# The last layer's key and value projections read x times the norm's weight, and its root enters behind them

## The reference, cut to what matters

```python
def rms_norm_2(x, g):
    xf = x.astype(jnp.float32)
    y = xf * lax.rsqrt(jnp.mean(xf * xf, axis=-1, keepdims=True) + EPS)
    return (y * g.astype(jnp.float32)).astype(x.dtype)

def shared_kv(h, norm_g, w_kv, knorm_g, cos, sin):
    Bsz, S, _ = h.shape
    kv = (rms_norm_2(h, norm_g) @ w_kv).astype(jnp.float32)
    k, v = jnp.split(kv, 2, axis=-1)
    k = k.reshape(Bsz, S, B_KV_HEADS, B_HD)
    v = v.reshape(Bsz, S, B_KV_HEADS, B_HD)
    k = apply_rope(rms_norm_2(k, knorm_g), cos, sin)
    return k, v
...
def dilated_layer(h, k, v, norm_g, w_in, qnorm_g, w_out, cos, sin):
    Bsz, S, _ = h.shape
    proj = rms_norm_2(h, norm_g) @ w_in
    q, z = jnp.split(proj, [B_QW], axis=-1)
```

## Time and profile before

| what | us |
|---|---|
| median of 3 runs (2129.85 to 2136.19) | 2133.31 |
| device time of the profiled execution | 2135.45 |
| its span, first to last instruction | 2133.7 |
| TensorE busy in the span | 1981.5 |
| VectorE busy | 1175.1 |
| ScalarE busy | 847.1 |

### The profile page before, as it was taken

The page is one execution under the profiler, slowest core; times in us unless marked ns, Lnnn a source line. Parts: engine busy times, 40 slices in busy tenths (PEclk is TensorE's granted clock), DMA queues, the critical chain, the costliest instruction groups (busy, mean ns, idle before and its releaser), DMA issues.

```text
span 2133.7 us, 24330 instructions
## 1 busy us (share of the span) xinstructions
PE 1981.5 (93%) x9296; PEld 1630.8 (76%) x9296; DVE 1175.1 (55%) x2051; ACT 847.1 (40%) x1319; POOL 0.2 (0%) x4
## 2 busy tenths in 40 slices
PE   1989988999998998889989999999999999899999
PEld 0866666888886887889877888887887877677877
DVE  8557846665667465466535432435653555655554
ACT  3226713232223533256633231324344534557343
POOL 0000000000000000000000000000000000000000
PEclk7999999999999979589999999999999999899999
DMA  9551053556554222000022222222221132132021
GB/s 357 202 207 41 1 186 140 208 177 214 179 200 154 99 79 79 1 1 1 1 90 79 99 98 98 98 98 79 88 90 60 60 143 79 59 119 79 1 90 59
DMA packets 42216, 223.85 MB, mean 105 GB/s; under 512 B 4444, under 2 KB 5212, under 8 KB 23694
## 3 DMA queue, kind: packets, MB, share of 16 engines
q1 hardware_dynamic: 41602, 222.25, 29.3%
q10 hardware_dynamic: 524, 0.41, 0.1%
HBM read 219.45 MB, written 3.19 MB: 104 GB/s over the span
## 4 chain that ended last, share of the span: by engine, by line
PE 83%; DVE 8%; DMA 4%; ACT 3%; issue 2%; SPq 0%; DVEq 0%; ACTq 0%
PE bank L419 22%; PE bank L421 22%; PE bank L420 22%; PE bank L1554 3%; DMA raw<-wts_d 2%; PE bank L1525 2%; DMA adab<-ada_d 1%; PE bank L1515 1%; PE bank L2701 1%; PE bank L1516 1%; DVE wL L405 1%; DMA ada<-ada_d 1%; DVE tmp L522 1%; PE bank L731 1%; ACT wH L400 1%
## 5 line engine op out<-in xcount | busy, mean ns | idle before, releaser
L419 PE MATMUL bank<-hH,wH 128*128 128x512 f32 x1344 | 536.8, 399 | 65.8 <-DVE hL L531 37.7
L420 PE MATMUL bank<-hL,wH 128*128 128x512 f32 x1344 | 531.3, 395 | 0.0
L421 PE MATMUL bank<-hH,wL 128*128 128x512 f32 x1344 | 531.2, 395 | 0.0
L419 PEld LDWEIGHTS bank<-hH,wH 128*128 128x128 f32 x1344 | 258.2, 192 | 129.8 <-issue 66.7
L996 ACT ACTIVATE wH<-raw 128x2048 fp32r<-128x2048 f32 x64 | 122.7, 1917 | 470.6 <-PE bank L421 470.6
L405 DVE TENSOR_TENSOR wL<-raw,wH 128x2048 fp32r<-128x2048 f32 x76 | 174.0, 2289 | 238.2 <-ACT wH L400 237.9
L420 PEld LDWEIGHTS bank<-hL,wH 128*128 128x128 f32 x1344 | 258.0, 192 | 54.4 <-issue 1.0
L421 PEld LDWEIGHTS bank<-hH,wL 128*128 128x128 f32 x1344 | 257.2, 191 | 54.8
L1040 DVE TENSOR_TENSOR wL<-raw,wH 128x2048 fp32r<-128x2048 f32 x64 | 146.5, 2289 | 228.8 <-ACT wH L996 228.8
L400 ACT ACTIVATE wH<-raw 128x2048 fp32r<-128x2048 f32 x76 | 145.3, 1912 | 259.6 <-PE bank L421 221.3
L419 PE MATMUL bank<-aH,wH 128*128 128x512 f32 x512 | 199.2, 389 | 0.0
(11 more groups left out here) (344 smaller groups left out, 2585.8 us busy)
## 6 DMA issues: line engine op xcount, KB each, us to landing
raw<-wts_d SPq DMA_DIRECT2D x140, 1024.0 KB, 4.9
adab<-ada_d SPq DMA_DIRECT2D x96, 512.0 KB, 4.3
ada<-ada_d SPq DMA_DIRECT2D x4, 2048.0 KB, 22.4
bt<-bias_rows SPq DMA_DIRECT2D x1, 4096.0 KB, 12.7
x<-x_d SPq DMA_DIRECT2D x1, 2048.0 KB, 9.5
peF<-ple_d SPq DMA_DIRECT2D x2, 1024.0 KB, 5.7
out_d<-x SPq DMA_DIRECT2D x4, 512.0 KB, 2.7
pF<-p_d SPq DMA_DIRECT2D x2, 512.0 KB, 3.6
```

The lines of the kernel that those rows point to most:

```text
L419: pe.matmul(o, l[0], r[0], start=start, stop=False)
L420: pe.matmul(o, l[0], r[1], start=False, stop=False)
L421: return pe.matmul(o, l[1], r[0], start=False, stop=stop)
```

## The change

Keys and values are now projected from x times the norm's weight, without the root of the mean square. The root r of a token is a common factor of its key and value. For the keys the norm of each head removes it again, if eps is divided by r squared: the program forms eps times the mean square plus eps squared (`epsK`, one VectorE instruction) and adds it to the head's mean square in place of eps (four VectorE instructions, which read PSUM and write kD). For the values the root is multiplied in where ScalarE copies them out, as a scale per token; for that TensorE transposes the root (four 128x128 transposes) and VectorE copies one column of each into `rtok`. Since the gate projection still reads hH and hL, chunks 4 to 7 of the new operand have a place of their own (k4H, k4L). The mean of the squares is taken after chunk 5 of the key tile, and the query norm's chunks 4 to 7 are applied first.

```diff
+        def xg(c):
+            return (hH[:, c, :], hL[:, c, :]) if c < 4 else (sb["k4H"][:, c - 4, :], sb["k4L"][:, c - 4, :])
+
+        def xg_act(act, c):
+            act.wait_ge(ple_x, c + 1)
+            act.activation(xg(c)[0], x[:, c, :], ACT.Copy, scale=col("norm_kv", c)).then_inc(h_hi, 1)
+
+        def xg_dve(dve, c):
+            dve.wait_ge(h_hi, KC * 7 + c + 1)
+            dve.scalar_tensor_tensor(out=xg(c)[1], in0=x[:, c, :], scalar=col("norm_kv", c),
+                                     in1=xg(c)[0].bitcast(F32), op0=ALU.mult, op1=ALU.subtract).then_inc(h_lo, 1)
...
             hi(act, n + 3)
-            if n + 4 < N_HALF:
+            if l == 0:
                 hi(act, n + 4)
+
+                act.wait_ge(half_used, n + 3)
+                for c in range(4):
+                    xg_act(act, c)
             for m in range(4):
                 o, freed = evac(act, a + 3, m)
                 bank_done(act, DONE0[a + 3], m, n + 4)
                 act.activation(sg[:, 4 + m, :], o, ACT.Sigmoid).then_inc(freed, 1)
-                if l == 0 and m < 3:
-                    sq_act(act, 7, lambda e, c: e.wait_ge(ple_x, c + 1), [m])
-            if n + 4 < N_HALF:
+                if l == 0 and m >= 1:
+                    xg_act(act, 3 + m)
+            if l == 0:
+                xg_act(act, 7)
                 act.preload_act_table_set(EXP_LN)
...
         def act_fourth(act):
-            sq_act(act, 7, lambda e, c: e.wait_ge(ple_x, c + 1), range(3, KC))
-            rstd_act(act, 7, 61)
-            apply_act(act, 7, None, lambda e: hi(e, N_K2 + 1))
+            hi(act, N_K2 + 1)
+            sq_act(act, 7, lambda e, c: e.wait_ge(ple_x, c + 1), range(KC))
             hi(act, N_K2 + 2)
+            rstd_act(act, 7, 60)
+            apply_act(act, 8, None, chunks=range(4, KC))
             hi(act, N_K2 + 3)
             act.wait_ge(half_used, N_K2 + 2)
             head_copy(act, 0)
 
             hi(act, N_DI)
             apply_act(act, 8, None, chunks=range(0, 4))
-            head_rstds(act, 0)
+            for m in range(4):
+                r = kD[:, m, :]
+                act.wait_ge(acc_free[1], 4 * 30 + m + 1)
+                act.activation(r, r, ACT.Ln).then_inc(ln_done, 1)
+                act.wait_ge(ln_done, 8 + m + 1)
+                act.activation(r, r, ACT.Exp, scale=-0.5).then_inc(hn_ex, 1)
             hi(act, N_DI + 1)
-            apply_act(act, 8, None, chunks=range(4, KC))
+            act.wait_ge(rp, 6)
             for m in range(4):
                 o, freed = evac(act, 62, m)
-                act.activation(vD[:, m, :], o, ACT.Copy).then_inc(freed, 1)
+                act.activation(vD[:, m, :], o, ACT.Copy, scale=rtok[:, m:m + 1]).then_inc(freed, 1)
...
         def dve_fourth(dve):
-            sq_dve(dve, 7, range(4, 7))
+            lo(dve, N_K2 + 1)
+            sq_dve(dve, 7, range(1, 7))
...
-            apply_dve(dve, 7, 7, lambda c: col("norm_kv", c), None, lambda e: lo(e, N_K2 + 1))
-            dve.wait_ge(rp, 4)
             lo(dve, N_K2 + 2)
+
+
+            dve.wait_ge(rstd_done, 8)
+            dve.tensor_scalar(sb["epsK"][:, :], bank[:, 0, :], EPS, EPS * EPS, ALU.mult, ALU.add).then_inc(rp, 1)
+            dve.wait_ge(l_t, 9)
+            dve.tensor_copy(rtok, blocks(bank[:, 3, :])[:, :, 0:1].rearrange("p i o -> p (i o)")).then_inc(rp, 1)
+            apply_dve(dve, 8, 7, lambda c: col("norm_b", c), None, chunks=range(4, KC))
+            dve.wait_ge(rp, 5)
             lo(dve, N_K2 + 3)
             head_rope(dve, 0)
             lo(dve, N_DI)
+            for m in range(4):
+                o, freed = evac(dve, 61, m)
+                dve.wait_ge(hn_mm, m + 1)
+                dve.scalar_tensor_tensor(out=kD[:, m, :], in0=o, scalar=float(D // P), in1=sb["epsK"][:, :],
+                                         op0=ALU.mult, op1=ALU.add).then_inc(freed, 1)
             apply_dve(dve, 8, 7, lambda c: col("norm_b", c), None, chunks=range(0, 4))
             head_end(dve, 0)
             lo(dve, N_DI + 1)
-            apply_dve(dve, 8, 7, lambda c: col("norm_b", c), None, chunks=range(4, KC))
             lo(dve, N_DI + 2)
...
         def pe_fourth(pe):
-            stats_pe(pe, 7, 61)
-            tile_mm(pe, 61, N_K2, hbase=56)
-            tile_mm(pe, 62, N_K2 + 2, tok=True, between=lambda: head_pe(pe, 0))
-            tile_mm(pe, 63, N_DI, hbase=64)
+            acc_wait(pe, 61)
+            for j in range(2):
+                pe.wait_ge(w_lo, N_K2 + j + 1)
+                for kk in range(4):
+                    k = 4 * j + kk
+                    pe.wait_ge(h_lo, KC * 7 + k + 1)
+                    for m in range(4):
+                        last = three(pe, bank[:, 4 + m, :], wpart((N_K2 + j) % 2, kk, m * P, P), xg(k), k == 0,
+                                     k == KC - 1)
+                    if k == 5:
+                        stats_pe(pe, 7, 60, 62)
+                last.then_inc(half_used, 1)
+            pe.wait_ge(rstd_done, 8)
+            for i in range(NT):
+                last = pe.transpose(bank[:, 3, i * P:(i + 1) * P], rstd[:, i * P:(i + 1) * P], ident[:, :])
+            last.then_inc(l_t, 1)
...
+            tile_mm(pe, 63, N_DI, hbase=68)
```

More of the change, by code:

```diff
@@ L320, in place @@
     m["dmask"] = nc.alloc_sbuf_tensor_at("dmask", [P, T], F32, offset=m["cw2_at"])
+    t("k4H", [P, 4, T], "bias", 8 * K, F32R)
+    t("k4L", [P, 4, T], "bias", 16 * K, F32R)
+    t("epsK", [P, T], "bias")
     t("rope", [P, 2, T], "misc", 12 * K)
@@ L452, in tile_mm @@
                     if hbase is not None:
-                        pe.wait_ge(h_lo, hbase + 4 * j + kk + 1)
+                        pe.wait_ge(h_lo, min(hbase + 4 * j + kk + 1, KC * 9) if a == 63 else hbase + 4 * j + kk + 1)
                     for m in range(4):
@@ L500, in sq_dve, with stats_pe @@
                 dve.tensor_tensor(sq_slot(0), sq_slot(0), sq_slot(c), ALU.add).then_inc(sq_sum, 1)
-        def stats_pe(pe, s, next_a):
-            acc_wait(pe, next_a)
+        def stats_pe(pe, s, next_a, after=None):
+            acc_wait(pe, after or next_a)
             if s == 0:
@@ L516, in rstd_act, with nth @@
             act.activation(rstd[:, :], bank[:, 4 * (next_a % 2), :], ACT.Ln, bias=one[:, 1:2]).then_inc(ln_done, 1)
-            act.wait_ge(ln_done, s + 1)
+            act.wait_ge(ln_done, s + 1 + (4 if s == 8 else 0))
             act.activation(rstd[:, :], rstd[:, :], ACT.Exp, scale=-0.5).then_inc(rstd_done, 1)
+        TMP0 = [KC * p if p < 8 else KC * (p - 1) for p in range(10)]
+        def nth(p, c):
+            return (c + 4) % KC if p == 8 else c
         def apply_dve(dve, p, s, scale, shift, mid=None, chunks=range(KC)):
             def product(c):
-                dve.scalar_tensor_tensor(out=tmp[:, c % 3, :], in0=x[:, c, :], scalar=scale(c), in1=rstd[:, :],
+                dve.scalar_tensor_tensor(out=tmp[:, nth(p, c) % 3, :], in0=x[:, c, :], scalar=scale(c), in1=rstd[:, :],
                                          op0=ALU.mult, op1=ALU.mult).then_inc(tmp_done, 1)
             def rest(c):
-                dve.wait_ge(h_hi, KC * p + c + 1)
+                dve.wait_ge(h_hi, KC * p + nth(p, c) + 1)
                 if shift is None:
-                    dve.tensor_tensor(hL[:, c, :], tmp[:, c % 3, :], hH[:, c, :].bitcast(F32),
+                    dve.tensor_tensor(hL[:, c, :], tmp[:, nth(p, c) % 3, :], hH[:, c, :].bitcast(F32),
                                       ALU.subtract).then_inc(h_lo, 1)
@@ L536, in slot_wait @@
             def slot_wait(c):
-                if c >= 3:
-                    dve.wait_ge(h_lo, KC * p + c - 2)
+                if nth(p, c) >= 3:
+                    dve.wait_ge(h_lo, KC * p + nth(p, c) - 2)
             for c in chunks[0:2]:
@@ L553, in apply_act @@
             for c in chunks:
-                act.wait_ge(tmp_done, KC * p + c + 1)
+                act.wait_ge(tmp_done, TMP0[p] + nth(p, c) + 1)
                 if shift is None:
-                    act.activation(hH[:, c, :], tmp[:, c % 3, :], ACT.Copy).then_inc(h_hi, 1)
+                    act.activation(hH[:, c, :], tmp[:, nth(p, c) % 3, :], ACT.Copy).then_inc(h_hi, 1)
                 else:
@@ L2440, in ple_dve @@
             lo(dve, n + 3)
-            if n + 4 < N_HALF:
+            if l == 0:
                 lo(dve, n + 4)
+                dve.wait_ge(ple_x, 4)
+                for c in range(4):
+                    xg_dve(dve, c)
             for c in range(4, KC):
                 gated(c)
-                if l == 0 and 5 <= c:
-                    sq_dve(dve, 7, [c - 4])
                 grow(c)
+                if l == 0 and c >= 5:
+                    dve.wait_ge(ple_x, c)
+                    xg_dve(dve, c - 1)
+            if l == 0:
+                dve.wait_ge(ple_x, KC)
+                xg_dve(dve, KC - 1)
         def ple_pe(pe, l, a, n, hbase):
@@ L2662, in head_end @@
                 dve.wait_ge(hn_ex, e + 1)
```

(29 more changed lines are left out.)

## The result

The changed kernel takes 2118.38 us (median of 7 runs, 2112.17 to 2125.03) against 2134.18 us before (7 runs). The ratio is 0.9926, with a 95% interval of 0.9908 to 0.9943: 12 to 20 us faster, 15.8 us between the medians. The forecast was 2119.2 us, 14.1 us less than before. The profiled execution has a span of 2117.5 us, 16.2 less than that of before.

The account below looks back on a forecast made before the run. TensorE was taken as the bound, busy 1981.5 of 2133.7 us, with two stalls. Filling the pause ahead of the keys brings the values' copies and tile 64 14.1 us earlier: 2133.31 - 14.1 = 2119.2 us, range 2114 to 2125.

Parts of the forecast that it names:

- The pause ahead of the keys: Between gate projection and key tile: keys follow at once, at 1814.95 instead of 1829.13, 14.18 us earlier.
- Statistics and transposes at full clock: Around the key tile: two statistics matmuls inside it, 1.73 us, plus four transposes, 0.44, so 2.17 us more.
- TensorE's side to tile 63: First query tile can start on TensorE 13.94 us earlier, at about 1864.3: 14.18 + 1.93 - 2.17.
- The chain to the values' copies: ScalarE and VectorE steps from the key tile's end, 36.2 us: copies end at 1874.65 against 1888.77, 14.1 us earlier.
- The scale per partition in the copies: ScalarE's four value copies: reading a scale per partition adds 4 x 0.087 = 0.35 us to 2.04.
- From the copies to tile 64: From the values' copies' end through two moves and the load: 15.97 us as before, so tile 64 at 1890.6.
- The slow start behind it: Slow matmuls behind tile 64's wait for its weights (some 4.5 us) stay; full clock there would save 1.7 us.
- The rule on transposes: Four transposes before the values: 0.44 us and nothing after by the rows; by the skill's rule possibly a 1.93 us slow start.
- Values' copies not earlier: Rival: the list ahead of the values' copies runs 14 us longer than summed, no change, 2133 us; chance 0.04.
- Slower by the clock: Rival: small waits keep TensorE at 1.2 GHz through key and value tiles, up to 43 us, 2162; chance 0.03.
- A wait inside the key tile: Rival: longer lists run 3 us late, TensorE waits 1 to 3 us in the key tile, 2122 to 2125; chance 0.10.
- Half of the second stall goes: Rival: before tile 64, up to 1.7 us or the whole 4.5 us wait also goes, 2113 to 2117; chance 0.05.

Follow-up runs that it names:

- e1: Changed kernel with the two statistics matmuls ahead of the key tile again, not behind its fifth chunk: ratio 1.0009 to the kernel before, stage 171.71 us.
- e5: Changed kernel with the two statistics matmuls two chunks earlier in the key tile (k == 3 for k == 5): ratio 0.9943 to the kernel before.
- e2: Changed kernel with the load of weight half N_DI+2 issued ahead of the values' move in SP's queue: 2113.11 us, ratio 0.9906 to the kernel before.
- e4: Changed kernel with VectorE's copy of the root per token put behind the query norm's chunks 4 to 7: ratio 0.9899 to the kernel before.
- e3: Kernel before the change, with the load of weight half N_DI+2 issued ahead of the values' move: ratio 0.9983 to the kernel before.
- e7: Changed kernel with both reorderings, e2's earlier load and e4's later root copy: 2112.26 us, ratio 0.9891 to the kernel before.
- e6: Changed kernel with the query norm's chunks 4 to 7 back in their old place, behind weight half N_DI+1: ratio 0.9945 to the kernel before.

## Why the prediction was right, point by point

- **The pause ahead of the keys.** Forecast: gone, 14.18 us. Measured: the last gate matmul and the first key matmul start 0.23 us apart (1812.53 and 1812.76), the pace of full speed. The forecast had let the keys begin behind the end of that last matmul, at 1814.95 on its clock; matmuls overlap (0.39 us long, 0.23 apart), so they came 0.22 us earlier. e1 puts the pause back, and the gain goes with it.
- **Statistics and transposes at full clock, 2.17 us.** From the first key matmul (1812.76) to the first transpose (1836.30) pass 23.54 us, and 96 x 0.2267 + 1.73 = 23.49.
- **TensorE's side to tile 63.** Forecast 60.2 us behind the anchor (1864.3 - 1804.11), measured 1862.00 - 1802.14 = 59.86; 0.22 of the difference is the start of the keys. The waits that the forecast feared where it had no margin did not occur: the last square of the heads was ready 50.2 us behind the anchor (paced: 50.6), the query norm's chunk 0 at 59.3 (paced: 60.0).
- **The chain to the values' copies.** Forecast: they begin 68.1 us behind the anchor. Measured 67.22, 0.87 earlier. Two terms were mis-sized, both for the better. The four pairs of Ln and Exp took 1.19 each, not 1.24; Ln takes 0.62 on kD, where it took 0.67 on PSUM with a second operand (`one`), and no run tells which of the two makes the difference. The four sums from PSUM took 2.39 to the next instruction, 0.60 each, where I had taken 0.66. These two make up 0.45; most of the rest was already there when ScalarE began to round N_DI (50.10 us behind the anchor, forecast 50.5), half of it from the earlier start of the keys. The sums on VectorE, then ScalarE, in the changed kernel:

```profile
1856.39 2.48 DVE L3023 SCALAR_TENSOR_TENSOR kD<-bank,epsK 128x512 f32<-128x512 f32 x4
1858.78 2.07 DVE L532 SCALAR_TENSOR_TENSOR tmp<-x,cols,rstd 128x512 f32<-128x512 f32 x3
...
1862.81 0.62 ACT L2977 ACTIVATE kD<-kD 128x512 f32<-128x512 f32 x1
1863.46 0.63 ACT L2979 ACTIVATE kD<-kD 128x512 f32<-128x512 f32 x1
1863.99 0.62 ACT L2977 ACTIVATE kD<-kD 128x512 f32<-128x512 f32 x1
...
1867.55 1.90 ACT L403 ACTIVATE wH<-raw 128x2048 fp32r<-128x2048 f32 x1
1869.36 2.40 ACT L2984 ACTIVATE vD<-bank,wr 128x512 f32<-128x512 f32 x4
```

- **The scale per partition in the copies.** Forecast 0.35 us more for four; measured 2.40 against 2.04.
- **From the copies to tile 64.** Forecast 15.97 as before; measured from 1871.76 to 1887.90, 16.14. Tile 64 started 85.76 us behind the anchor, against 100.63 before: 14.87 us earlier, where the forecast had 14.1.
- **The slow start behind it.** Forecast unchanged at 1.7 us. It cost 2.3: 11 matmuls took 4.83 us (the stretch from 1887.90 above) where 2.49 is full speed. This gave back most of the 0.8 us that the chain had gained, so that the total of 14.15 fits the forecast of 14.1 better than its parts do. That is luck, and so is a part of the agreement in time (2118.38 for 2119.2): the forecast stood on a median of 2133.31 for the kernel before, and its seven runs gave 2134.18.
- **The rule on transposes.** Through the values, right behind four transposes, the clock is 1.00. As forecast from the rows, they cost their own time, 0.45 us, and nothing after. The Trainium skill (TensorE: Matmul & The Clock Gate, Part 4) says that they do not count for the clock gate as matmuls do; this trace shows that four among matmuls bring no fall.
- **The rivals.** "Values' copies not earlier": they came 15.4 us earlier against the anchor (82.6 to 67.2). "Slower by the clock": clock 1.00 over keys and values. "A wait inside the key tile": none, and e5 shows what it would have cost. "Half of the second stall goes": not in the changed kernel, but e2 and e4 show both ways to have it, each worth the wait and its slow start.

## What to carry to other kernels

In this kernel the norm ahead of a projection held TensorE up by 14.2 us, for square, sum, root and application. Where the root can be applied behind the projection, the projection can start on x times the weight, and the statistics go inside it at the first place where they are ready; two chunks too early cost 3.8 us (e5). Then follow the new list on the other engines: here one chain held up tile 64, and two links of it could be taken out. One small VectorE copy stood in line waiting for TensorE and delayed the values' copies, and one weight load stood behind their move in SP's queue. Moving either was worth 6 us of this stage, and moving both no more, since either takes the whole wait. Compare executions from an anchor inside them, since 2 us of the difference of two spans lay where nothing was changed.

## What the runs showed that I had not expected

How long TensorE runs at the lower clock after a pause differs for nearly the same pause. Behind 4.54 us of wait 12 matmuls took 4.42 us, 1.7 more than at full clock; behind 3.98 us of wait 11 took 4.83 us, 2.3 more; and in e5, behind 3.87 us at the same place, nine took 3.71 us, 1.7 more. The Trainium skill (TensorE: Matmul & The Clock Gate, Part 1, What's actually happening) says that the count differs from run to run, which agrees. A wait of 2.91 us was enough for slow matmuls behind it (e5).

Moving e2's line shortened the stage by 6.5 us on either kernel, but the medians moved by 3.2 us (e3) and 5.3 us (e2). The part behind the scores took 160.1 to 160.4 us in five traces and 161.7 to 161.9 in the four others. Both e2 and e3 are among the four, but so are e5 and e7, and e5 does not have that line. In the four traces whose waits I compared there (changed kernel, e2, e4 and e7), TensorE's waits in that part are nearly the same. Its granted clock is not. In the 35 us that begin 40 us behind the first score TensorE is busy throughout, and the clock is 0.94 (e2, e5) and 0.95 (e3, e7) in the longer ones, against 0.97 (e6), 0.98 (changed kernel, e1) and 0.99 (kernel before, e4) in the shorter. Between e2 and the changed kernel that is some 1.4 us (an estimate: 35 x 0.04) of the 1.7 that they differ by. So the longer ones have more time at the lower level there; why stays open.
